# A two-layer decoder trunk in 32-bit parts: how the second head group's queries and keys are made

## The reference, cut to what matters

```python
def mixer_attention(x, w_in, b_f, w_out, rel_bias):
    h = x @ w_in
    qkv_a = h[..., :3 * wa].reshape(B, S, 3, N_HEADS_A, HEAD_DIM).transpose(2, 0, 3, 1, 4)
    qkv_b = h[..., 3 * wa:3 * wa + 3 * wb].reshape(B, S, 3, N_HEADS_B, HEAD_DIM).transpose(2, 0, 3, 1, 4)
    ...
    o_a = moba_attention(qkv_a[0], qkv_a[1], qkv_a[2], rel_bias)
    o_b = forgetting_attention(qkv_b[0], qkv_b[1], qkv_b[2], log_f)
    o = jnp.concatenate([o_a, o_b], axis=1).transpose(0, 2, 1, 3).reshape(B, S, D_ATTN)
    return o @ w_out
```

## Time and profile before

| | before |
|---|---|
| median of three runs | 998.75 us (998.64 to 999.25) |
| the profiled execution's own time | 998.70 us |
| its span, first to last instruction | 997.0 us |
| PE busy | 991.9 us (99%) |
| DVE busy | 703.7 us (71%) |
| ACT busy | 458.3 us (46%) |
| DMA, mean | 192 GB/s |
| granted TensorE clock, mean | 1.00 |

### The profile page before, as it was taken

How to read it: one execution, slowest core, us unless ns; L and a number is a source line. 1 busy time by engine, 2 the same in 40 slices (tenths; PEclk the granted TensorE clock), 3 DMA queues, 4 the chain that set the end, 5 groups by cost and what they waited for, 6 DMA issues and landing times.

```text
span 997.0 us, 13952 instructions
## 1 busy us (share of the span) xinstructions
PE 991.9 (99%) x5370; PEld 850.7 (85%) x5370; DVE 703.7 (71%) x876; ACT 458.3 (46%) x524; POOL 49.7 (5%) x74
## 2 busy tenths in 40 slices
PE   9999999999999999999999999999999999999998
PEld 7888888889878888888888888888898888888887
DVE  5866666878678766666786666668787876666684
ACT  5444344246574544444445443434354553434441
POOL 0700000100001000000010000000210000000010
PEclk9999999999999999999999999999999999999999
DMA  8965656466264675555457755555466676565531
GB/s 289 289 234 168 211 168 212 133 191 185 85 212 164 201 245 192 188 191 194 143 170 270 230 183 201 180 199 182 145 205 218 215 243 213 168 212 171 211 128 43
DMA packets 129799, 191.45 MB, mean 192 GB/s; under 512 B 5448, under 2 KB 95816, under 8 KB 129760
## 3 DMA queue, kind: packets, MB, share of 16 engines
q1 hardware_dynamic: 126432, 180.11, 54.5%
q0 software_dynamic: 3040, 10.54, 3.1%
q10 hardware_dynamic: 288, 0.26, 0.1%
HBM read 189.83 MB, written 1.06 MB: 191 GB/s over the span
## 4 chain that ended last, share of the span: by engine, by line
PE 99%; DMA 0%; DVE 0%; issue 0%; DVEq 0%
PE gu L619 26%; PE gu L627 14%; PE acc L435 10%; PE acc L436 10%; PE acc L437 10%; PE gu L435 6%; PE gu L437 5%; PE gu L436 5%; PE tp L534 2%; PE gu L829 2%; PE gu L919 2%; PE gu L810 2%; PE gu L834 1%; PE gu L924 1%; PE gu L813 1%; PE acc L754 1%
## 5 line engine op out<-in xcount | busy, mean ns | idle before, releaser
L619 PE MATMUL gu<-xT,g_hi 128*128 128x512 f32 x1152 | 274.6, 390 | 0.0
L619 PEld LDWEIGHTS gu<-xT,g_hi 128*128 128x128 f32 x1152 | 215.5, 188 | 44.5 <-ACT g_hi L987 0.2
L1472 DVE TENSOR_REDUCE stage<-gu 128x256 f32<-128x512 f32 x72 | 49.8, 691 | 146.0 <-PE gu L627 146.0
L627 PEld LDWEIGHTS gu<-xT,g_lo 128*128 128x128 f32 x1152 | 147.7, 191 | 5.6
L627 PE MATMUL gu<-xT,g_lo 128*128 128x256 f32 x1152 | 149.4, 283 | 0.0
L1323 DVE TENSOR_TENSOR g_lo<-rawA,g_hi 128x2048 fp32r<-128x2048 f32 (+2 forms) x63 | 136.8, 2173 | 17.4 <-ACT g_hi L987 17.2
L1323 DVE TENSOR_TENSOR g_lo<-rawB,g_hi 128x2048 fp32r<-128x2048 f32 (+1 forms) x64 | 136.5, 2134 | 7.4 <-ACT g_hi L987 7.3
L435 PE MATMUL acc<-d_hi,hT_hi 128*128 128x512 f32 x352 | 138.6, 394 | 0.0
L436 PE MATMUL acc<-d_lo,hT_hi 128*128 128x512 f32 x352 | 137.9, 392 | 0.0
L437 PE MATMUL acc<-d_hi,hT_lo 128*128 128x512 f32 x352 | 137.0, 389 | 0.0
L987 ACT ACTIVATE g_hi<-rawA 128x2048 fp32r<-128x2048 f32 (+2 forms) x64 | 116.0, 1816 | 40.6 <-DMA rawA<-in_ffn_w_up 16.0
(11 more groups left out here) (205 smaller groups left out, 1020.9 us busy)
## 6 DMA issues: line engine op xcount, KB each, us to landing
rawD<-in_ffn_w_down SPq DMA_DIRECT2D x44, 1024.0 KB, 5.5
rawA<-in_ffn_w_gate SPq DMA_DIRECT2D x42, 512.0 KB, 4.0
rawA<-in_ffn_w_up SPq DMA_DIRECT2D x42, 512.0 KB, 5.0
rawB<-in_ffn_w_gate SPq DMA_DIRECT2D x42, 512.0 KB, 4.0
rawB<-in_ffn_w_up SPq DMA_DIRECT2D x42, 512.0 KB, 5.0
rawA<-in_attn_w_in SPq DMA_DIRECT2D x12, 512.0 KB, 4.4
rawB<-in_attn_w_in SPq DMA_DIRECT2D x12, 512.0 KB, 4.5
rawA<-in_ple_w_gate SPq DMA_DIRECT2D x8, 512.0 KB, 4.8
```

The costliest lines, as they stand in the source:

```text
L619: pe.matmul(bank[:, :], g_hi[:, slot, b, at:at + P], xT[:, b, :, :].rearrange("p i t -> p (i t)"), start=b == 0, stop=False)
L627: done = pe.matmul(bank[:, 0:S], g_lo[:, slot, b, at:at + P], xT[:, b, 0, :], start=False, stop=b == KB - 1)
L1472: dve.tensor_reduce(gates, gu[0][:, :].rearrange("p (i t) -> p t i", i=2), AXX, ALU.add).then_inc(gate_sum, 1)
```

## The change

The chunks 3 and 4 (queries and keys of group b) are made in the wide form too, so no step is narrow any more. Their sums are DVE's work now, and ACT's copies of them are gone. The queries' scale goes into chunk 3's weights. The low parts of the chunks 4 and 5, which DVE made at the steps ("g", 3, h) and ("g", 4, h), become entries of their own, ("low", c, h), which stand behind the scores and exponentials of the same stretch and ahead of the inverse.

```diff
 ATTN_COLS = [2, 0, 1, 3, 4, 5]
-WIDE = 2
-WIDE_STEPS = {(1, 0): ("low", 0, 1), (1, 1): (0, 1, "low"), (2, 0): (0, 1, "low"), (2, 1): (0, "low", 1)}
+WIDE = 4
+WIDE_STEPS = {(1, 0): ("low", 0, 1), (1, 1): (0, 1, "low"), (2, 0): (0, 1, "low"), (2, 1): (0, "low", 1),
+              (3, 0): (0, 1), (3, 1): (0, 1), (4, 0): (0, 1), (4, 1): (0, 1)}
 ATTN_ORDER = [
     ("g", 0, 0), ("g", 0, 1), ("forget",),
     ("g", 1, 0), ("exp",), ("g", 1, 1), 
     ("g", 2, 0), ("pT", 0), ("g", 2, 1), ("log",),
-    ("g", 3, 0), ("pT", 1), ("scores", 0), ("exps", 0), ("inverse", 0),
-    ("g", 3, 1), ("probs", 0), ("probs", 1), ("scores", 1), ("exps", 1), ("values", 0), ("inverse", 1), ("cum",),
-    ("g", 4, 0), ("probs", 2), ("probs", 3), ("scores", 2), ("exps", 2), ("values", 1), 
+    ("g", 3, 0), ("pT", 1), ("scores", 0), ("exps", 0), ("low", 3, 0), ("inverse", 0),
+    ("g", 3, 1), ("probs", 0), ("probs", 1), ("scores", 1), ("exps", 1), ("values", 0), ("low", 3, 1), ("inverse", 1), ("cum",),
+    ("g", 4, 0), ("probs", 2), ("probs", 3), ("scores", 2), ("exps", 2), ("low", 4, 0), ("values", 1),
     ("outputs", 0, 0), ("inverse", 2),
-    ("g", 4, 1), ("probs", 4), ("probs", 5), ("scores", 3), ("exps", 3), ("inverse", 3),
+    ("g", 4, 1), ("probs", 4), ("probs", 5), ("scores", 3), ("exps", 3), ("low", 4, 1), ("inverse", 3),
     ("g front", 5, 0), ("values", 2), ("probs", 6), ("probs", 7), ("g back", 5, 0),
...
@@ -1161,8 +1162,8 @@
-                            elif c == 0 and WIDE:
-                                hi_scaled(g0 + 1, h)
+                            elif c in (0, 2):
+                                hi_scaled(g0 + c + 1, h)
...
@@ -1608,12 +1609,16 @@
                             elif 1 <= c <= WIDE:
                                 for part in WIDE_STEPS[c, h]:
-                                    if part == "low":
+                                    if part == "low" and c == 2:
+                                        lo_scaled_rows(g0 + 3, h, slice(0, 4)).then_inc((split_a, split_b)[h], 1)
+                                    elif part == "low":
                                         lo_g(g0 + c + 1, h)
                                     else:
                                         qk_sum(c, h, part)
                             else:
                                 lo_g(g0 + c + 1, h)
+                        elif e[0] == "low":
+                            lo_g(g0 + e[1] + 1, e[2])
```

## The result

The changed kernel takes 1000.13 us (median of 22 runs, 999.74 to 1000.65) against 998.62 for the kernel before, measured beside it (22 runs, 998.25 to 999.25). That is +1.51 us, a ratio of 1.0015 with a 95% interval of 1.0009 to 1.0021. The forecast was 1000.0, +1.27, from 998.5 to 1001.1.

A forecast was written before the change was run, and what follows sets the result against it. PE was taken to bound the kernel, busy 991.9 of 997.0 us. Waits of 0.97 and 1.14 us less a saving of 0.84 gave +1.27 us, so 1000.0 us, range 998.5 to 1001.1.

The forecast's parts named there:

- The two waits: PE waits for bank 1's sum inside step (3, 0), 0.97 us, and before transposes of heads 6 and 7, 1.14 us.
- The second wait: At pair 3, PE waits for DVE before transposes: 0.84 us for head 6, 0.30 for head 7, 1.14 us together.
- One of the signs of being wrong: PE's start of the values of group b ("g front", 5, 0) not within 0.4 us of 260.4.
- PE's saving: Four wide steps replace narrow ones in chunks 3 and 4, each saving 0.21 us, 0.84 us in all.
- ACT loses four copies: In the changed stretch ACT has four copies fewer; no time was counted for it.
- rival 3: Wide form brings PE next to nothing here, saving 0.16 us by the skill's spacing: +1.95, 1000.7 us; chance 0.05.
- The chain of DVE in between: DVE's unbroken 14 us from 244.3 to 258.8: no wait, margins 0.7 and 0.4 us (heads 4, 5), 0.6 (bank 0).
- a possible third wait: At PE's transposes of heads 4 and 5, if DVE's chain is later than the 0.4 us margin.
- Rival 2: Third wait at transposes of heads 4 and 5; with 1.6 us of DVE lateness +2.5, 1001.2 us; chance 0.09.
- rival 1: DVE covers everything and PE just gains: 997.9 us; chance 0.09 for no wait, 0.10 for one.
- rival 4: New waits lower PE's clock; 1.2 GHz for one step costs another 5.6 us, 1005.7 us; chance 0.02.
- The loads: Chunk 5's halves are fetched later, the first landing at 245.1 us; costed at nothing.

The follow-up runs named there:

- e1: Changed kernel with both of DVE's sums of step (2, 1) ahead of the low part: 998.93 us, +0.31 against the kernel before.
- e2: Changed kernel with transposes of heads 6 and 7 behind g back (5, 0), pair 4's scores ahead of pair 3's values: 998.98 us, +0.36 over the kernel before.
- e3: Changed kernel with the edits of e1 and e2 together: 998.12 us, -0.50 against the kernel before.
- e8: Against e3, the low part of chunk 5's second half moved right behind the sums of (4, 1): 997.81 us, -0.82 against the kernel before.
- e6: Changed kernel with four small memsets on DVE behind the cumulative term, delaying it 1.45 us: 1001.40 us, +2.77 over the kernel before.
- e4: Changed kernel with narrow steps again, low parts of chunks 4 and 5 kept in their new place: 1000.56 us, +1.94 over the kernel before.
- e7: Kernel before, with both sums of step (2, 1) ahead of the low part: 999.32 us, +0.69.

## Why the prediction was right

**The two waits.** Both stand where they were put, released by the instruction that was named. Step (3, 0) was to take 6.61 us and took 6.66. The second wait was to cost 1.14 us and cost 1.24 (1.38 - 0.14). e1 and e2 take away one each, and by the traces 1.03 and 0.97 us go (medians 1.20 and 1.15); e3 takes away both, and 1.96 go (2.01). So by the traces they add up (2.00 against 1.96), and together they are more than the whole loss; the medians, 2.35 against 2.01, agree within what they can tell.

Inside the two waits the account is this. For the first, the forecast let PE ask for bank 1 at 230.93, wait 0.97 us and pay the slow first matmul once. In the trace both blocks begin with one (229.66 to 229.98, and 232.44 to 232.79, against 0.23 in a run), so PE asked about 0.1 us later, waited about 0.86 and paid twice: two errors of 0.1 us that cancel. For the second, the 0.1 us that the forecast lacks are there to 0.07 in the lateness of head 6 (0.91 against 0.84): reading a pair takes 1.56 us (261.07 to 262.63), not 1.50. The difference between +1.38 by the trace and +1.51 by the medians is left open; the runs can't resolve it.

One of the signs of being wrong did appear as it was written: the values of group b begin at 260.97, not within 0.4 us of 260.4. Of these 0.57 us, 0.54 lie ahead of the change, in the late first loads; counted from ("pT", 0) the start is off by 0.03. The sign should have been a distance, not a time of the span.

**PE's saving.** The sum had 0.84 us. The runs show 0.82 (e8) and the traces 0.83 to 0.88, but it is made otherwise: 0.18 to 0.19 for each step, not 0.21 (a wide step after other work takes 5.67 us, I had read 5.64 off step (2, 1)), and the rest from the copies that ACT no longer has ahead of the probabilities. "ACT loses four copies" was costed at nothing, and what waited behind them was not asked: right sum, one term 0.1 too large and one left out, which is luck. The forecast's 0.228 us for a wide matmul was also misread: 3.62/16 is 0.226. With 0.120 for a narrow one, as the long runs of both traces have it, a pair saves 13 ns and not 11.

The spacing by the Trainium skill, "TensorE: Matmul & The Clock Gate", section "Back-to-back issue gap", would have made the saving 0.16 us. The section gives this spacing for an isolated matmul and says itself that it does not hold for a stream of matmuls with their weight loads, so it should not have been put forward as a rule for this stream. By e3 and e8 the four steps give 0.74, and rival 3 is refuted.

**The chain of DVE in between.** No other wait came, as worked out. Head 5 was to be ready 0.4 us ahead of PE and was 0.27 (258.91 + 0.55 = 259.46 against the transposes' start at 259.36 and 0.37 more), and bank 0 of step (4, 1) 0.5 instead of 0.6. Where I named the place of a possible third wait I chose the smaller margin, heads 4 and 5. e6 shows that for a lateness that arises ahead of the sums there are two places: PE meets the bank first and loses 1.1 us there; being late itself it then loses only 0.3 at head 5 and nothing at head 4. Rival 2's mechanism was right and its place right for the smaller part; it left out the bank.

**The other rivals.** That DVE covers everything (rival 1) is refuted by e1 and e2. The granted clock stayed at 1.00 in the kernel after, through waits of 0.9 us, so rival 4 did not occur. The loads came late and cost PE nothing, as costed: ACT's longest wait for one in the waits view of 203 to 300 us is 2.0 us in both kernels, and PE has none.

## What to carry to other kernels

On a kernel whose PE never idles, price a change by lateness and not by load: walk through the engines' written-out orders with durations from the trace, and for each operand write down when it is ready and when PE first asks for it. A new form of a product changes what it asks for first (here a second bank after 1.9 us, and low parts not before 3.7 in place of 2), so the order of the helper engine must be turned with it. Here two places did not fit: the order of the sums of (2, 1), left as it was, cost 1.0 us, and the new place of the last low part, with the transposes left where they stood, cost 1.2, against a saving of 0.8. And a halved change can be worse than either end: both parts of this one alone cost more than the whole.

## What the runs showed that I had not expected

The first matmul after a wait, or after a matmul of another kind, holds the next one back: 0.31 to 0.34 us from start to start in place of 0.23 for 512 columns. It isn't only there: in e3, where nothing waits, the first matmul of step (3, 0) comes right behind low matmuls of the same tiles and still holds the next back (229.16 to 229.49). What sets it was not tested. The wait of 0.86 us in step (3, 0) thus costs 1.0. And the walk through the list by hand was good to 0.1 us beside its ranges in six of eight expectations, though in e6 it missed the place of the greater wait. The misses are e4 (0.3 us), where I took the late half of an operand to be the one asked for first, and e7 (0.5 us), where I did not walk through the list at all.
